# A two-layer attention block: the low halves of a turned head pair ahead of a weight conversion, and three gated heads in one slot

## The reference

```python
        hn = rmsnorm(h, norm_gain[l])
        proj = hn @ w_in[l]
        dq, dk, dv, dg, fq, fk, fv, ff, fg = jnp.split(proj, split_points, axis=-1)
        ...
        do = diff_attention(dq, dk, dv, lam, chunk_ids)
        do = rmsnorm(do, subln_gain[l], SUBLN_EPS) * (1.0 - lam_init)
        do = jnp.transpose(do, (0, 2, 1, 3)).reshape(b, lp, DIFF_WIDTH)
        do = do * jax.nn.silu(dg)
        ...
        fo = forgetting_attention(fq, fk, fv, cum_logf, positions)
        fo = jnp.transpose(fo, (0, 2, 1, 3)).reshape(b, lp, FOX_WIDTH)
        fo = fo * jax.nn.silu(fg)
        h = h + jnp.concatenate([do, fo], axis=-1) @ w_out[l]
```

## Time and profile before

| | |
|---|---|
| runs | 1751.77, 1749.59, 1750.78 us |
| median | 1750.78 us |
| the profiled execution | 1750.99 us, span 1749.2 us, so 1.79 us lie around the span |
| mean granted TensorE clock | 0.967 of full |
| PE busy | 1624.8 us (93%) |
| DVE busy | 1229.8 us (70%) |
| ACT busy | 1039.2 us (59%) |
| POOL busy | 63.8 us (4%) |

### The profile page before, as it was taken

One profiled execution on the slowest core, in us unless ns is written; L12 is line 12 of the kernel. 1 busy time (PEld: TensorE's weight loads), 2 busy tenths in 40 slices (PEclk: granted clock), 3 DMA queues, 4 the chain that ended last, 5 costly groups with the idle time before them and its releaser, 6 DMA issues.

```text
span 1749.2 us, 21555 instructions
## 1 busy us (share of the span) xinstructions
PE 1624.8 (93%) x8649; PEld 1362.7 (78%) x8649; DVE 1229.8 (70%) x1298; ACT 1039.2 (59%) x1247; POOL 63.8 (4%) x64
## 2 busy tenths in 40 slices
PE   5997999988869999999999999999997989889987
PEld 5875888877758888888888888888886877788866
DVE  3655455357648888888888888888886566555665
ACT  4644444345537776777677777677676456454463
POOL 0000000011110000000000000000000200003000
PEclk9999999988969999999999999999998999899989
DMA  7422555552118999999999999999996643236410
GB/s 246 145 97 96 162 176 192 188 188 97 53 55 310 392 345 346 326 330 389 321 351 325 368 362 336 337 310 402 318 352 166 132 121 97 49 77 139 124 47 37
DMA packets 133080, 389.30 MB, mean 223 GB/s; under 512 B 8694, under 2 KB 14266, under 8 KB 132844
## 3 DMA queue, kind: packets, MB, share of 16 engines
q1 hardware_dynamic: 132692, 387.15, 65.4%
q10 hardware_dynamic: 280, 0.69, 0.1%
HBM read 386.77 MB, written 1.05 MB: 222 GB/s over the span
## 4 chain that ended last, share of the span: by engine, by line
PE 79%; DVE 9%; ACT 7%; issue 4%; DMA 0%; ACTq 0%; DVEq 0%; SPq 0%; POOL 0%
PE psum L354 25%; PE psum L356 24%; PE psum L355 23%; DVE wlo L189 4%; ACT whi L179 4%; PE psum L1493 1%; PE psum L1545 1%; DVE Ss L1192 1%; PE psum L413 1%; DVE mx L1197 1%; PE psum L2211 1%; PE psum L2197 0%; ACT hh L1604 0%; PE psum L2056 0%; ACT sil L1599 0%
## 5 line engine op out<-in xcount | busy, mean ns | idle before, releaser
L189 DVE TENSOR_TENSOR wlo<-raw,whi 128x2048 fp32r<-128x2048 f32 (+1 forms) x286 | 629.0, 2209 | 239.6 <-ACT whi L179 238.8
L179 ACT ACTIVATE whi<-raw 128x2048 fp32r<-128x2048 f32 (+1 forms) x286 | 526.3, 1847 | 250.7 <-PE psum L356 250.7
L354 PE MATMUL psum<-whi,xh 128*128 128x512 f32 (+1 forms) x1280 | 497.1, 388 | 15.9 <-DVE xl L2557 7.9
L356 PE MATMUL psum<-whi,xl 128*128 128x512 f32 (+1 forms) x1280 | 486.0, 380 | 0.0
L355 PE MATMUL psum<-wlo,xh 128*128 128x512 f32 (+1 forms) x1280 | 485.1, 379 | 0.0
L354 PEld LDWEIGHTS psum<-whi,xh 128*128 128x128 f32 x1280 | 242.3, 189 | 72.7 <-DVE wlo L189 12.6
L356 PEld LDWEIGHTS psum<-whi,xl 128*128 128x128 f32 x1280 | 242.0, 189 | 49.5
L355 PEld LDWEIGHTS psum<-wlo,xh 128*128 128x128 f32 x1280 | 242.5, 189 | 45.9 <-issue 0.2
L189 DVE TENSOR_TENSOR wlo<-raw_more,whi 128x2048 fp32r<-128x2048 f32 (+1 forms) x94 | 204.1, 2178 | 40.3 <-ACT whi L179 39.8
L179 ACT ACTIVATE whi<-raw_more 128x2048 fp32r<-128x2048 f32 (+1 forms) x94 | 171.3, 1827 | 53.8 <-PE psum L356 53.8
L354 PE MATMUL psum<-xh,whi 128*128 128x256 f32 (+2 forms) x552 | 164.5, 298 | 16.8 <-DVE wlo L189 15.2
(11 more groups left out here) (367 smaller groups left out, 1537.5 us busy)
## 6 DMA issues: line engine op xcount, KB each, us to landing
raw<-in_moe_w_down_dram SPq DMA_DIRECT2D x58, 1024.0 KB, 7.7
raw<-in_moe_w_gate_dram SPq DMA_DIRECT2D x43, 1024.0 KB, 6.3
raw<-in_moe_w_up_dram SPq DMA_DIRECT2D x41, 1024.0 KB, 6.1
raw_more<-in_moe_w_down_dram SPq DMA_DIRECT2D x30, 1024.0 KB, 7.8
raw<-in_w_in_dram SPq DMA_DIRECT2D x28, 1024.0 KB, 8.0
raw_more<-in_moe_w_up_dram SPq DMA_DIRECT2D x23, 1024.0 KB, 5.3
raw_more<-in_moe_w_gate_dram SPq DMA_DIRECT2D x21, 1024.0 KB, 6.7
raw<-in_moe_w_up_dram SPq DMA_DIRECT2D x23, 768.0 KB, 5.5
```

The source lines that it names most:

```text
L179: act.e.activation(self.whi[:, i % self.ns, 0:kt * n], self.place[self.slots[i]][:, 0:kt * n], ACT.Copy, scale=1.0).then_inc(self.s_hi)
L189: dve.e.tensor_tensor(self.wlo[:, i % self.ns, 0:kt * n], self.place[self.slots[i]][:, 0:kt * n], self.whi[:, i % self.ns, 0:kt * n].bitca ...
L354: pe.e.matmul(o, lh, rh, start=start, stop=False)
L356: return pe.e.matmul(o, ll, rh, start=False, stop=stop)
```

## The change

Two things change in `att_order`, for both layers. In slot `nd+3` the call of `low` stands after `turned` instead of ahead of it. In slots `nd+4` and `nd+5` the counts are 3 and 2 instead of 2 and 3.

```diff
-    N_BESIDE_F = ((2, 2, 2, 0, 2, 3) + (1,) * 9, (2, 2, 2, 0, 2, 3) + (1,) * 5)
+    N_BESIDE_F = ((2, 2, 2, 0, 3, 2) + (1,) * 9, (2, 2, 2, 0, 3, 2) + (1,) * 5)
...
-            low()
+            if u != nd + 3:
+                low()
             take(beside, n // 2)
             if 0 <= u - 2 < nu:
                 turned(u - 2)
+            if u == nd + 3:
+                low()
             take(beside, n - n // 2)
```

## The result

| | before | changed |
|---|---|---|
| median | 1750.78 us (10 runs) | 1754.53 us (10 runs) |
| lowest to highest | 1749.05 to 1753.22 | 1752.68 to 1756.89 |
| profiled execution | 1750.99, span 1749.2 | 1752.69, span 1750.9 |
| mean granted clock in it | 0.967 | 0.965 |

The ratio is 1.0019, with a 95% interval of 1.0010 to 1.0027: 3.3 us slower (1.8 to 4.7). The forecast was 1752.4, in a range of 1749.0 to 1755.4. The sign and the mechanism on VectorE came out as replayed; the size is about twice the replayed one, and the experiments are mostly about this second half.

A forecast was written before the change was run, and what follows sets the result against it. VectorE and ScalarE's chain into `out(0)` was taken as the bound: 0.90 - 0.12 = +0.78 us a layer, +1.56 together on 1750.99 gives 1752.55, stated as 1752.4 since the median is 0.2 lower; range 1749.0 to 1755.4.

The forecast's parts named there:

- What bounds: Both layers: the chain over VectorE and ScalarE in turn sets the start of `out(0)`, and everything later moves with it.
- Part A: Slot `nd+3`, `aTl` ahead of the conversion: VectorE waits for `aTh`, so `out(0)` starts 0.90 us later a layer.
- earlier turning: TensorE's turning of unit `nd+2` starts 1.3 us earlier; forecast to bring nothing, as a rival passed on to `out(0)`: 1748.1, 6%.
- Part B: Slots `nd+4` and `nd+5`, head 2 gated earlier and head 3 earlier: 0.87 - 0.99 = -0.12 us a layer.
- the step from the end of `xl` to gate 2: VectorE, slot `nd+4`: the step after `xl` of head 0, as gate 2 waits for it, taken as 0.04 us.
- The new wait of TensorE: Turning head 2 needs bank 6, so TensorE waits about 2.9 us for gate 0; no overrun into `out(0)` in the sum.
- The clock, "I leave the term as it is": Half clock at the start of `out(0)` costs nine matmuls 0.2 each, 1.8 us a layer, taken as unchanged.
- The sum: Both layers: 0.90 - 0.12 = +0.78 each, together +1.56 on 1750.99, so 1752.55, stated as 1752.4 for the median.
- the slower rival: Clock returns a spell later, behind the start of `out(0)`: 1.7 us a layer, 1755.9 in all; 13%.
- The faster rivals: Two cases below the forecast: the clock holds to `out(0)`, 1748.9, 8%; TensorE's earlier turning is passed on, 1748.1, 6%.
- The clock that holds: TensorE's first idle shrinks from 2.27 to 1.0, so full clock survives to `out(0)`: gain 1.8 a layer, 1748.9; 8%.

The follow-up runs named there:

- late conversion: Changed kernel with the conversion moved from slot `nd+3` to slot `nd+5`, behind `xl` of head 3: median 1748.09 us, ratio 0.9972 to the kernel before.
- plain delay: Kernel before with two idle subtractions of 450 columns on VectorE ahead of `xl` of head 3: median 1754.54 us, ratio 1.0016.

## Why the prediction was right, and where it was off

- **What bounds.** Right. The start of `out(0)` decides, and VectorE and ScalarE set it. The late conversion moved it by all of its 2.20 us, and the plain delay reproduced the change.
- **Part A, +0.90 a layer.** Right: +0.89 and +0.91 alone. VectorE waited 0.82, and TensorE's earlier turning, which came with a wait of 0.97 instead of 2.27, didn't reach `out(0)`. (The view names ScalarE as what ended that wait; `aTl` ended at the same 1478.72 + 0.96 = 1479.68, and by the code it is `aTl` that this turning waits for.)
- **Part B, -0.12 a layer.** Sign right, size less than half: -0.05 and -0.04 alone. The term that was off is the step from the end of `xl` to gate 2, which I took as 0.04; it is 1486.43 + 0.43 = 1486.86 to 1486.97, so 0.11.
- **The new wait of TensorE.** Forecast about 2.9, found 2.85, and its overrun into `out(0)` didn't happen.
- **The clock, "I leave the term as it is".** This is the step that failed. The sum gave 1752.4, the measurement 1754.5. I treated the clock as a constant 1.8 us a layer with scatter, and put its getting worse aside as the slower rival with 13%. It got worse, in part of the executions: 7 us more at half clock on the mean, and the spell at 1728. That is the rival's mechanism at half of its price of 3.4: behind `out(0)` the profiled execution took 1.6 us more in the two layers, where the sum had nothing. The range held because it was drawn to take in one layer of it; that the measurement fell inside says nothing for the sum.
- **The faster rivals.** The clock that holds did not come by the change; six idle matmuls brought it back by the start of `out(0)`. The earlier turning was not passed on.

## What to carry to other kernels

Ahead of moving a short operation in front of a long one, compare the start of the long one with the end of what the short one waits for: VectorE paid that difference, 0.9 us, for everything behind. An earlier result is worth nothing if the engine that takes it up is held by something else, as ScalarE was here. A long operation that is not due belongs into the engine's long wait for the bottleneck; here that was 6 us wide and two slots away. In this kernel, where TensorE's clock fell behind waits of 2 to 5 us, a change of its start time was paid at about twice its replayed size, and filling the wait helped beyond the noise in one kernel of four. Elsewhere the factor has to be measured: compare the time at half clock behind the moved start, not over the whole execution.

## What the runs showed of the hardware

- A wait of TensorE of the same length may or may not bring the clock down: 2.12 us in layer 1 left it at 1.00 before and, as 2.13 us, brought it to 0.50 at 1728 in the changed kernel. The clock fell behind 2.27 us of waiting, although matmuls were running again by then.
- How long it stays down behind `out(0)`'s start differs: about 4 us in the kernel before, 6.1 in layer 1 of the changed one, with the same work on TensorE.
- In these traces half clock costs time only where TensorE is what the rest waits for: about 0.4 us for each 1 us behind `out(0)`, nothing in the stretch from `aTh` to `out(0)`, where VectorE and ScalarE set the pace.
- Matmuls that compute nothing can pay for themselves: six of them, 2.8 us at half clock, took 5 us off the changed kernel. The 1 us or less that they took off the late conversion, the kernel before and the kernel with the delay is inside the noise.
- Executions of one kernel spread by 4 to 12 us wherever there were ten or more of them, and the mean granted clock goes with the time.
